# Block-product sums of a gated feed-forward layer: from GpSimd to VectorE, all as two-operand instructions

## The reference, cut to what matters

```python
def swiglu(x, w_gu, w_down):
    g, u = jnp.split(x @ w_gu, 2, axis=-1)
    return (jax.nn.silu(g) * u) @ w_down
...
        u = modulate(rmsnorm(h, norm3_g[l]), mod[:, 2, 0], mod[:, 2, 1])
        h = h + FFN_RES_WEIGHT * mod[:, 2, 2][:, None, :] * swiglu(u, ffn2_w_gu[l], ffn2_w_down[l])
```

## Time and profile before

| | |
|---|---|
| median of 3 runs | 2042.84 us (2042.66 to 2042.88) |
| the profiled execution, its own time | 2042.68 us |
| its span, first to last instruction | 2041.4 us |
| outside the span | 1.28 us |
| TensorE busy | 2006.2 us, 98% |
| VectorE busy | 1196.0 us, 59% |
| ScalarE busy | 894.9 us, 44% |
| GpSimd busy | 366.4 us, 18% |

### The profile page before, as it was taken

The page is one execution under the profiler, slowest core; times in us unless marked ns, Lnnn a source line. Parts: engine busy times, 40 slices in busy tenths (PEclk is TensorE's granted clock), DMA queues, the critical chain, the costliest instruction groups (busy, mean ns, idle before and its releaser), DMA issues.

```text
span 2041.4 us, 25850 instructions
## 1 busy us (share of the span) xinstructions
PE 2006.2 (98%) x10133; PEld 1712.2 (84%) x10133; DVE 1196.0 (59%) x1721; ACT 894.9 (44%) x1282; POOL 366.4 (18%) x261
## 2 busy tenths in 40 slices
PE   7999999999999998999999999999999999999998
PEld 5888888888888888999898888888888888888888
DVE  6665555624565668568476455544376575564666
ACT  5322222435656545445255455554434343342344
POOL 4000000001101223122120354443000021020130
PEclk8999999999999999999999999999999999999999
DMA  7855653532223532423233433333535333233232
GB/s 304 277 195 186 201 190 117 165 111 77 79 78 104 181 103 84 131 77 122 85 100 107 151 109 114 111 107 124 184 115 166 102 105 102 93 97 99 85 109 75
DMA packets 84393, 261.42 MB, mean 128 GB/s; under 512 B 9248, under 2 KB 13472, under 8 KB 84272
## 3 DMA queue, kind: packets, MB, share of 16 engines
q1 hardware_dynamic: 84272, 259.77, 40.0%
HBM read 242.92 MB, written 16.81 MB: 127 GB/s over the span
## 4 chain that ended last, share of the span: by engine, by line
PE 92%; DVE 3%; ACT 3%; issue 1%; DMA 0%; POOL 0%; SPq 0%; DVEq 0%; ACTq 0%; POOLq 0%
PE P L909 29%; PE P L910 29%; PE P L911 29%; PE P L1129 1%; PE P L1410 1%; PE P L1141 1%; PE P L1140 1%; ACT WH L754 0%; PE P L1022 0%; DVE SQ L2294 0%; DVE TL L2665 0%; PE P L1457 0%; DVE SL L2587 0%; DMA H<-x 0%; DVE WL L772 0%
## 5 line engine op out<-in xcount | busy, mean ns | idle before, releaser
L909 PE MATMUL P<-UH,WH 128*128 128x512 f32 (+1 forms) x1687 | 639.3, 379 | 5.5 <-POOL UL L3243 4.2
L910 PE MATMUL P<-UL,WH 128*128 128x512 f32 (+1 forms) x1687 | 635.2, 377 | 0.0
L911 PE MATMUL P<-UH,WL 128*128 128x512 f32 (+1 forms) x1687 | 635.1, 376 | 0.0
L754 ACT ACTIVATE WH<-WRAW 128x1024 fp32r<-128x1024 f32 (+2 forms) x324 | 330.9, 1026 | 593.8 <-PE P L911 590.1
L909 PEld LDWEIGHTS P<-UH,WH 128*128 128x128 f32 x1687 | 318.2, 189 | 63.6 <-issue 6.1
L911 PEld LDWEIGHTS P<-UH,WL 128*128 128x128 f32 x1687 | 318.1, 189 | 58.3
L910 PEld LDWEIGHTS P<-UL,WH 128*128 128x128 f32 x1687 | 318.3, 189 | 55.9
L772 DVE TENSOR_TENSOR WL<-WRAW,WH 128x1024 fp32r<-128x1024 f32 (+1 forms) x228 | 285.2, 1254 | 131.7 <-ACT WH L754 131.1
L787 POOL TENSOR_TENSOR WL<-WRAW,WH 128x1024 fp32r<-128x1024 f32 x59 | 143.4, 2431 | 349.5 <-ACT WH L754 349.5
L909 PE MATMUL P<-AH,WH 128*128 128x512 f32 x500 | 195.1, 390 | 0.0
L910 PE MATMUL P<-AL,WH 128*128 128x512 f32 x500 | 194.6, 389 | 0.0
(11 more groups left out here) (330 smaller groups left out, 3230.4 us busy)
## 6 DMA issues: line engine op xcount, KB each, us to landing
WRAW<-w_gu SPq DMA_DIRECT2D x88, 512.0 KB, 3.6
ADA<-w_ada SPq DMA_DIRECT2D x72, 512.0 KB, 4.7
WRAW<-w_down SPq DMA_DIRECT2D x48, 512.0 KB, 3.6
WRAW<-w_up SPq DMA_DIRECT2D x44, 512.0 KB, 3.5
WRAW<-w_in SPq DMA_DIRECT2D x40, 512.0 KB, 3.5
WRAW<-w_mix SPq DMA_DIRECT2D x36, 512.0 KB, 3.6
WRAW<-w_down SPq DMA_DIRECT2D x24, 384.0 KB, 3.2
WRAW<-w_out SPq DMA_DIRECT2D x16, 512.0 KB, 3.8
```

Source lines behind the costliest of these rows:

```text
L754: s.act.activation(hi, self.raw(item), FN.Copy).then_inc(*self.rounded.inc(item))
L909: pe.matmul(out, wh, xh, start=start, stop=False, skip_group_check=True)
L910: pe.matmul(out, wh, xl, start=False, stop=False, skip_group_check=True)
L911: return pe.matmul(out, wl, xh, start=False, stop=stop, skip_group_check=True)
```

## The change

All sums move to VectorE as `tensor_tensor` (two operands), and `pool_second` is deleted. The first token sum is issued inside `dve_norm`, after `lower(5)`; the other three in `dve_second` after the remainder of up 1. For each of the 19 tiles, `dve_first_sums` makes s3 and s1: before `dve_sums` for tiles 3, 8 and 16, and in the loop of `dve_quads` between the remainder of up f and `glu(f-1)`. The remainders that were three-operand instructions become two-operand ones. The signal `forms` goes and its events join `comb`.

```diff
-            if self.beside_pool(item):
-                s.dve.scalar_tensor_tensor(lo, self.raw(item), 1.0, hi.bitcast(F32), OP.mult,
-                                           OP.subtract).then_inc(*self.low_v.inc(item))
-                continue
             s.dve.tensor_tensor(lo, self.raw(item), hi.bitcast(F32), OP.subtract).then_inc(
                 *self.low_v.inc(item))
...
         lower_all(i)
+        if name == "mix" and i == 5:
+            on.wait_ge(*s.snap("u full", 3))
+            dve.tensor_tensor(mem.form(1), mem.form(3), mem.form(1), OP.subtract).then_inc(
+                *s.comb.inc("t", 1))
...
+    def total(t, x, y):
+        dve.tensor_tensor(mem.form(t), mem.form(x), mem.form(y), OP.subtract).then_inc(
+            *s.comb.inc("t", t))
+
+    W.low(W.up(1))
+    on.wait_ge(*s.snap("u full", KD - 1))
+    on.wait_ge(*s.comb("t", 1))
+    total(3, 2, 3)
+    on.wait_ge(*s.comb("t", 3))
+    total(2, 2, 1)
+    on.wait_ge(*s.comb("t", 2))
+    total(4, 4, 2)
     W.low(W.gate(2))
     form(1)
     form(3)
...
     W.low(W.gate(3))
+    dve_first_sums(s, 3)
     dve_sums(s, 3)
...
             elif m == 6:
+                dve_first_sums(s, f)
                 dve_sums(s, f)
                 W.low(("sb", f))
...
+def dve_first_sums(s, f):
     mem, W, on, dve = s.mem, s.W, s.on_dve, s.dve
     gate, up = mem.WRAW[:, W.gate(f) % 4, :], mem.WRAW[:, W.up(f) % 4, :]
-    on.wait_ge(*s.forms("s3", f))
+    on.wait_ge(*W.loaded[W.gate(f) % 4](W.gate(f)))
     on.wait_ge(*W.loaded[W.up(f) % 4](W.up(f)))
-    dve.scalar_tensor_tensor(mem.SB[:, LEFT:RIGHT], up[:, RIGHT:D], 1.0, mem.SA[:, RIGHT:D],
-                             OP.mult, OP.subtract).then_inc(*s.comb.inc("s2", f))
+    if f != QUADS[0][0]:
+        on.wait_ge(*W.ready(("sa", f - 1)))
+    else:
+        on.wait_ge(*s.ep_lo(1, 1))
+    dve.tensor_tensor(mem.SA[:, RIGHT:D], gate[:, LEFT:RIGHT], up[:, LEFT:RIGHT],
+                      OP.subtract).then_inc(*s.comb.inc("s3", f))
+    dve.tensor_tensor(mem.SA[:, LEFT:RIGHT], up[:, LEFT:RIGHT], up[:, RIGHT:D],
+                      OP.add).then_inc(*s.comb.inc("s1", f))
...
         W.low(W.up(f))
+        if f != fs[-1]:
+            dve_first_sums(s, f + 1)
         if f != fs[0]:
             glu(f - 1)
...
-def pool_second(s):
```

More of the change, by code:

```diff
@@ L355, in __init__ @@
         self.v_lo = new("v_lo", [(*kind, tb) for kind in kinds[:3] for tb in range(4)])
-        comb = [("t lo", t) for t in (1, 3, 2, 4)]
+        comb = [("t", 1), ("t", 3), ("t", 2), ("t", 4), ("t lo", 1), ("t lo", 3), ("t lo", 2),
+                ("t lo", 4)]
         for fs in QUADS:
-            comb += [("s2", fs[0]), ("s4", fs[0]), ("c11", fs[0])]
+            comb += [(x, fs[0]) for x in ("s3", "s1", "s2", "s4", "c11")]
             for f in fs:
@@ L362, in __init__ @@
                 if f != fs[-1]:
-                    comb += [("s2", f + 1), ("s4", f + 1), ("c22", f), ("c11", f + 1)]
+                    comb += [(x, f + 1) for x in ("s3", "s1", "s2", "s4")]
+                    comb += [("c22", f), ("c11", f + 1)]
                 else:
@@ L408, in __init__ @@
         self.merged = new("merged", [(m,) for m in tiles])
-        self.forms = new("forms", [("t", t) for t in (1, 3, 2, 4)] +
-                         [(x, f) for fs in QUADS for f in fs for x in ("s3", "s1")])
         self.kl_zero = new("kl_zero", [("a",), ("b",)])
@@ L666, in low_on_pool @@
         return 0 < item < 6 or kind in ON_POOL or kind in HALF_ON_POOL and item % 2 == 1
-    def beside_pool(self, item):
-        return self.at_item[self.at["ffn2", "up", 1]] <= self.at_item[item] < \
-            self.at_item[self.at["ffn2", "down", 2, 0]]
     def ready(self, item):
@@ L720, in raw_ready @@
         if isinstance(item, tuple):
-            return self.s.forms("s1", item[1]) if item[0] == "sa" else self.s.comb("s4", item[1])
+            return self.s.comb("s1", item[1]) if item[0] == "sa" else self.s.comb("s4", item[1])
         return self.loaded[item % 4](item)
@@ L1901, in form @@
     def form(t):
-        on.wait_ge(*s.forms("t", t))
+        on.wait_ge(*s.comb("t", t))
         act.activation(mem.TH[:, t - 1], mem.form(t), FN.Copy).then_inc(*s.snap.inc("t hi", t))
@@ L2662, in form @@
     def form(t):
-        on.wait_ge(*s.forms("t", t))
+        on.wait_ge(*s.comb("t", t))
         on.wait_ge(*s.snap("t hi", t))
-        dve.scalar_tensor_tensor(mem.TL[:, t - 1], mem.form(t), 1.0,
-                                 mem.TH[:, t - 1].bitcast(F32), OP.mult, OP.subtract).then_inc(*s.comb.inc("t lo", t))
+        dve.tensor_tensor(mem.TL[:, t - 1], mem.form(t), mem.TH[:, t - 1].bitcast(F32),
+                          OP.subtract).then_inc(*s.comb.inc("t lo", t))
     def glu(e, f):
         dve_glu(s, "ffn2", e, f, mem.AH2, mem.AL2, mem.SIL2)
+    def total(t, x, y):
[9 more added lines that the diff above has]
+    total(4, 4, 2)
     W.low(W.gate(2))
@@ L2701, in dve_second @@
         down(p, KD - 1)
+def dve_first_sums(s, f):
+    mem, W, on, dve = s.mem, s.W, s.on_dve, s.dve
+    gate, up = mem.WRAW[:, W.gate(f) % 4, :], mem.WRAW[:, W.up(f) % 4, :]
+    on.wait_ge(*W.loaded[W.gate(f) % 4](W.gate(f)))
+    on.wait_ge(*W.loaded[W.up(f) % 4](W.up(f)))
+    if f != QUADS[0][0]:
[6 more added lines that the diff above has]
+                      OP.add).then_inc(*s.comb.inc("s1", f))
 def dve_sums(s, f):
@@ L2708, in dve_sums @@
     gate, up = mem.WRAW[:, W.gate(f) % 4, :], mem.WRAW[:, W.up(f) % 4, :]
-    on.wait_ge(*s.forms("s3", f))
-    on.wait_ge(*W.loaded[W.up(f) % 4](W.up(f)))
-    dve.scalar_tensor_tensor(mem.SB[:, LEFT:RIGHT], up[:, RIGHT:D], 1.0, mem.SA[:, RIGHT:D],
-                             OP.mult, OP.subtract).then_inc(*s.comb.inc("s2", f))
+    on.wait_ge(*s.comb("s3", f))
+    if f != QUADS[0][0]:
+        on.wait_ge(*W.ready(("sb", f - 1)))
+    dve.tensor_tensor(mem.SB[:, LEFT:RIGHT], up[:, RIGHT:D], mem.SA[:, RIGHT:D],
+                      OP.subtract).then_inc(*s.comb.inc("s2", f))
     on.wait_ge(*s.comb("s2", f))
-    dve.scalar_tensor_tensor(mem.SB[:, RIGHT:D], gate[:, RIGHT:D], 1.0, mem.SB[:, LEFT:RIGHT],
-                             OP.mult, OP.subtract).then_inc(*s.comb.inc("s4", f))
+    dve.tensor_tensor(mem.SB[:, RIGHT:D], gate[:, RIGHT:D], mem.SB[:, LEFT:RIGHT],
+                      OP.subtract).then_inc(*s.comb.inc("s4", f))
 def dve_quads(s, p):
@@ L2758, in lower @@
         on.wait_ge(*s.a_hi("ffn2", f))
-        dve.scalar_tensor_tensor(mem.AL2[:, j, :], mem.SIL2[:, f % 2, :], 1.0,
-                                 mem.AH2[:, j, :].bitcast(F32), OP.mult, OP.subtract).then_inc(*s.a_lo.inc("ffn2", f))
+        dve.tensor_tensor(mem.AL2[:, j, :], mem.SIL2[:, f % 2, :], mem.AH2[:, j, :].bitcast(F32),
+                          OP.subtract).then_inc(*s.a_lo.inc("ffn2", f))
     W.low(W.gate(fs[0] + 1))
@@ L3384, in pool_engine @@
     pool_mixer(s)
-    pool_second(s)
     pool_fox(s)
```

## The result

The changed kernel takes 2038.61 us (median of 10 runs, 2036.63 to 2039.57); the kernel before takes 2042.82 us (10 runs, 2040.70 to 2043.40). The ratio is 0.9979, 95% interval 0.9970 to 0.9989: 4.2 us or 0.21% faster. The forecast was 2039.4 in a range of 2037.4 to 2041.3. The profiled execution took 2038.94 us with a span of 2037.4 us.

The account below looks back on a forecast made before the run. VectorE's chain, hindered by GpSimd's sums, was taken to set TensorE's 5.6 us wait in ffn2. 4.6 won less 1.2 for added sums is 3.4; 2042.68 - 3.4 = 2039.3, median 2039.4 us, range 2037.4 to 2041.3.

Parts of the forecast that it names:

- What bounds: In ffn2, TensorE's one large wait, 5.6 us before m6 of tile 3, comes from VectorE's chain, stretched by GpSimd's sums.
- The chain in the norm and behind it: VectorE from the norm to the glu product of tile 0: that product starts 4.6 us earlier, despite the added token sums.
- The weight sums ahead of m6: Two 128x512 sums added to VectorE's chain before `dve_sums(3)` cost 1.2 us, leaving 3.4 us net.
- The loop: Loop over block products: VectorE takes some 9.6 us a tile of TensorE's 10.08, so the added sums cost nothing.
- The form: VectorE's remainders written with two operands for three: costed at nothing (0.68 against 0.69 us).
- The clock: TensorE's clock at the stall before m6: still falls after 2.8 us of idleness and costs 1.6 us as before.
- the other fate: Clock stays up at the stall before m6, so 1.6 us come back too: 2037.8 us; chance 0.28.
- A: Stall before m6 shrinks to 2.8 us and the clock still falls: 2039.4 us, the forecast; chance 0.55.
- B: Clock stays up at the stall before m6, winning 1.6 us more: 2037.8 us; chance 0.28.
- a change too small to tell: Whole kernel: a measured difference within about 0.2%, 4.1 us, of no change; chance 0.62, against 0.32 for faster.
- C: Clock falls at 788.8, stays low 6.7 us with TensorE at work, losing 3.35 us, not 1.6: 2041.2 us; chance 0.11.

Follow-up runs that it names:

- The run with a wait of 1.8 us: Changed kernel with the first token sum moved out of the norm to behind its last remainder, where VectorE idles; 2037.42 us (0.9976 to before).
- the token sums alone: Changed kernel with the 38 weight sums s3 and s1 back on GpSimd, the four token sums staying on VectorE; 2039.83 us (0.9989 to before).
- sums of one column: Kernel before with GpSimd's 42 sums cut to one column each, waits and signals kept, output not the reference's; 2035.33 us (0.9966 to before).
- three sums moved by a few lines: Changed kernel with the first token sum and s3 and s1 of tile 3 moved into VectorE's idle stretches; 2034.40 us (0.9960 to before).

## Why the prediction was right, by its steps

**What bounds.** Right. The only large wait in ffn2 was set by VectorE's chain, shown by five kernels whose m6 moved as the sums of VectorE's and ScalarE's instructions said: 1.00 for 1.0, 0.98 for 0.9, 5.6 for 5.5, 1.25 for 1.2, and 0.87 for 1.15.

**The chain in the norm and behind it.** First glu product 4.6 us earlier; measured from the norm's sums, 776.82 - 744.13 = 32.69 became 771.81 - 743.79 = 28.02: 4.67. The token sums took VectorE's price (1.22 us long, 763.61 to 767.27 for three, 3.66 us where 3.67 was forecast), not GpSimd's.

**The weight sums ahead of m6.** 1.2 us; they took 1.2, and 0.07 of it came back in a shorter wait. The sum of 3.4 us was 3.54.

**The loop.** 9.6 us a tile forecast, 9.51 measured; `glu` 1.0 us later; no wait. The slack was real but small: one more 128x512 instruction a tile costs nothing that can be told, two cost 5.5 us.

**The form.** Costed at nothing; it costs nothing, beside GpSimd too.

**The clock.** Forecast: it falls, at the price of before, with 0.28 for the other fate. One of three profiled executions of the changed kernel kept the clock up, and one of two of the kernels with more sums in the loop. That A and B are two fates of one kernel is shown; that the profiled execution laid beside the forecast met A is luck. Their shares aren't shown. Seven of the ten runs of the changed kernel lie at 2038.0 or above and three at 2036.6 to 2036.8, which looks like the two fates, but the start of the program alone moves a run by up to 2 us, and the kernel before has runs at 2040.7 and 2041.3 beside its median of 2042.8 as well. But the reason that I gave for A was wrong: I compared 2.8 us with the 2.4 of one row, as if a length of idleness decided. The run with a wait of 1.8 us lost the clock, and the changed kernel with 2.7 kept it once. C didn't show in any profiled execution of the changed kernel: where the clock fell at 788.5, it was back at 791.8. Its mechanism is real: with the token sums alone the clock stayed low for 6.8 us, 5.7 of them with TensorE at work, and that cost 2.5 us in place of 1.5.

**The result.** The measured 4.2 us are the 3.5 of the chain and 0.7 that I can't place. Runs in which the clock stayed up and the start of the program, which moves single runs by up to 2 us, are both large enough; which of them it is stays open. The gain is a hair above what can be told from no change, where I had given 0.62 to a change too small to tell.

The Trainium skill, page "SBUF — State Buffer", section "Who interferes with whom", calls the pair of ports that VectorE and GpSimd share an exclusive lock held for a whole instruction. The traces agree: GpSimd's sum at 762.27 ends at 764.67, and VectorE's remainder, issued at 763.17, ends at 765.75, 1.08 us after that the earlier trace rows. By the rule a collision is a wait for the other's instruction and no share of bandwidth. What the runs show either way is that it vanishes wholly with the neighbour's work: remainders of 1.22 us in the changed kernel and in the one with sums of one column.

## What to carry to other kernels

An engine with little to do is not a free place for work if its instructions stretch those of the engine that sets the pace: compare lengths of the same instruction with the neighbour busy and idle before costing a move. What counts is where the collision falls: 36 of the 42 moved instructions lay where slack hid them and gave nothing; six lay on the chain into a stall, and the four token sums among them gave 2.54 of the 3.54 us. And once work must be added to an in-order chain, put it into its idle stretches: three sums moved by a few lines brought m6 another 2.1 us forward, kept the clock up in the execution profiled, and gave about as much again as the whole change.

## What the runs showed of the hardware that I had not expected

- TensorE's clock fell (2.4 to 1.2 GHz) behind a wait of 1.8 us, 1.4 us after work had resumed, and stayed up in two of five executions behind one of 2.7 us. Behind waits of 0.6 and 0.7 us it stayed up in the one execution profiled of each. One profile tells one fate only.
- The low clock costs by the work that falls into it and not by its length: 6.8 us of it cost 1.6 us where TensorE stood still in nearly half of them (before), 2.5 where it worked in 5.7 of them (token sums alone), and 3.4 us with work in all of them cost 1.5 (changed).
- Two VectorE instructions of which the second needs the first's result start 0.71 us apart (779.24 to 779.95), independent ones 0.60 (778.03 to 778.63): the wait costs 0.11 us, where the Trainium skill, page "VectorE: DVE Perf Modes", section "The DRAIN you can't avoid", has a semaphore cost nothing extra.
